# FFN's gate and up tiles as seven half products of summed halves, in a two-block kernel on one Trainium2 core

## The chip, the cores and the metric

The kernel runs on one core of a Trainium2 chip: TensorE (matrix products, PE), VectorE (DVE), ScalarE (ACT), GpSimd (POOL), SyncE (SP, which here only issues DMAs), on-chip memory (SBUF), and eight accumulation banks of 128 x 512 fp32 that TensorE writes (PSUM). The metric is the device time of one execution in microseconds (us), without the profiler; lower is better.

## The reference

Two transformer-like blocks in float32 on x of [1, 512, 1024]: first a convolution branch, a differential attention and a cross attention, merged and projected; then a second block with gated mixing, a recurrent time mix, and FFN. Only FFN is touched:

```
x = layer_norm_2(ALPHA * x + gt1 * mix, ln1_g, ln1_b)
h = x * (1.0 + sc2) + sh2                     # [512, 1024]
gu = h @ w_ffn_in                             # [512, 2 * 2816]
f = (silu(gu[..., :2816]) * gu[..., 2816:]) @ w_ffn_out
x = layer_norm_2(ALPHA * x + gt2 * f, ln2_g, ln2_b)
```

## The kernel before, in words

Every large product is kept near fp32 by a split. An fp32 operand is rounded to the type fp32r (its hi part, by a ScalarE copy), and the rest, operand minus hi, is a second fp32r tile (its lo part, by a VectorE subtraction). `mm3` (lines 583 to 585) then issues three matmuls, hi x hi, hi x lo and lo x hi, into one bank.

Weights come as units of 128 x 1024 fp32 (512 KB) in the order of a written-out plan, through four `raw` slots; SyncE loads a slot again when its unit's lo part is done. `feed_hi` and `feed_lo` (lines 625 and 633) split the units in turn into three pairs of parts (SPLIT = 3), each freed when the product that used it is done. The engines run written-out instruction orders and wait on semaphores; a `Ring` hands out banks and scratch tiles in turn and waits for the last reader of each. Each engine takes its instructions strictly in its own order, so an instruction that waits holds all behind it.

FFN has 22 pairs of tiles. Pair n is the unit ffn_g n and the unit ffn_u n, each the 128 columns of one tile for all 1024 inputs (KT = 8 slices of 128 x 128). For each, TensorE multiplies the 8 slices with the 8 slices of h3_T (h transposed, hi and lo, 512 tokens): 24 matmuls of 512 columns into one bank of a ring of three (`units`). Pair 0 is computed in halves of 256 tokens while h3_T is still being turned (`first_units`). ScalarE takes the gate with Silu into a scratch tile, VectorE multiplies it by the up bank in place, ScalarE rounds the result (hidden hi, line 2152), VectorE makes its rest (hidden lo, line 2174). At n = 10 TensorE also makes gate rows (line 1492), which take two banks of the same ring; their input tiles come from `dve_diagonals` (line 2825). In pairs 2 to 5 VectorE also applies the first row norm's gains and biases (`dve_gain_rows`).

Then come 22 output products, one per unit ffn_out n: VectorE scales the raw weights by the gate rows (line 661), they are split, and TensorE adds 24 matmuls of 512 columns (4 token tiles x 2 halves x 3) into all eight banks, which stay taken until the end. The last three units are ordered by token tile, and the last norm runs behind it.

The modulated rows of h (h3) pass through three scratch tiles (`modulated_ring`), where ScalarE writes them, rounds them, and VectorE makes the rest. GpSimd does nothing in FFN but issue eight DMAs of norm rows.

Of the kernel before, what the change touches and what calls it, by code (L numbers as in the profile page):

```python
# [14 lines left out]
P = 128  # L15
# [30 lines left out]
HEAD_STEPS = {6: 1, 7: 3, 8: 2, 9: 2, 10: 2, 11: 2, 12: 2, 13: 2, 14: 2}  # L46
ROW_SPOT = {"emb": "even", "ln1": "odd", "ln2": "even", "sg": "sg"}
# [229 lines left out]
def build(nc, dram, out):  # L277
# [3 lines left out]
    in_turn = [u for u in weights_of if plan[u][0] not in EARLY]  # L281
# [161 lines left out]
    wide = bank_ring((0, 1, 2, 4, 5, 6, 7))  # L443
    half_places, last_places = bank_ring((0, 1, 2, 3)), bank_ring((3, 4, 5, 6, 7, 0, 1, 2))
# [13 lines left out]
    act_ring, modulated_ring = place_ring((0, 1, 2, 3)), place_ring((2, 3, 4))  # L458
# [3 lines left out]
    final_ring = place_ring((), (scratch[7], *scratch[0:4]))  # L462
    f_logw, f_wall, f_total, s_sq = scratch[0], scratch[3], scratch[5], scratch[4:6]
# [106 lines left out]
    hidden_hi, hidden_lo = signal("ffn_hi"), signal("ffn_lo")  # L570
# [40 lines left out]
    def feed_hi(act, count=1):  # L611
        for _ in range(count):
            n = progress["hi"]
            if n == len(weights_of):
                return
            progress["hi"] += 1
            u = weights_of[n]
            act.wait_ge(*(weight_scaled.at(u) if plan[u][0][0] == "ffn_out" else raw_loaded[u % RAW].at(u)))
# [2380 lines left out]
```

## Time and profile before

| what | us |
|---|---|
| median of 3 runs without the profiler | 1617.43 (1616.83 to 1620.52) |
| profiled execution: span from first to last instruction | 1726.6 |
| profiled execution: its time outside the span | not given |
| TensorE matmuls busy in the span | 1692.6 (98%) |
| TensorE weight loads busy | 1289.1 (75%) |
| VectorE busy | 1001.7 (58%) |
| ScalarE busy | 718.1 (42%) |
| GpSimd busy | 189.8 (11%) |

A matmul's row lasts longer than its share of the engine, as matmuls overlap in the pipeline: distances between starts tell the pace. Names of tiles in the rows are the program's; a region of memory that is reused shows the first name it had, so that FFN's h3_T appears as h_T. The granted clock is the share of TensorE's full speed that the chip let it have.

### The profile page before, as it was taken

How to read it: one execution, taken by the hardware profiler on the slowest of the kernel's cores; microseconds unless marked ns; L12 is line 12 of the kernel's file. 1: busy time of each engine (PE TensorE's matmuls, PEld its weight loads, DVE VectorE, ACT ScalarE, POOL GpSimd, SP SyncE). 2: the span in 40 equal slices, each digit the busy share in tenths (PEclk: the TensorE clock that was granted, in tenths of full speed). 3: DMA queues.
4: the chain of work that ended last, by engine and by line, in shares of the span. 5: the costliest groups of instructions: out<-in, count | busy, mean ns of one | idle time of the engine just before them, and what ended most of it. 6: DMA issues, size and time to landing. Idle time of an engine off the chain costs nothing.

```text
span 1726.6 us, 24370 instructions
## 1 busy us (share of the span) xinstructions
PE 1692.6 (98%) x9964; PEld 1289.1 (75%) x9964; DVE 1001.7 (58%) x1684; ACT 718.1 (42%) x1151; POOL 189.8 (11%) x159
## 2 busy tenths in 40 slices
PE   7999999999999999999999999989999999999998
PEld 6777776777777777777777877778768777777776
DVE  5999884566554477656444737675446442334335
ACT  5544356334422476647522535553324222222112
POOL 2335364300010000000005000000000000000000
PEclk9888888888888888888888888888888888888888
DMA  5223243543454322232324132200012232222221
GB/s 200 89 84 117 79 134 103 179 133 123 146 174 134 110 90 82 75 108 86 122 86 154 57 97 74 85 4 4 3 49 98 85 110 85 86 86 90 93 85 49
DMA packets 45645, 166.07 MB, mean 96 GB/s; under 512 B 5264, under 2 KB 5392, under 8 KB 45536
## 3 DMA queue, kind: packets, MB, share of 16 engines
q1 hardware_dynamic: 42912, 155.95, 28.3%
q0 software_dynamic: 2624, 8.59, 1.7%
q8 instruction: 79, 1.29, 0.3%
q14 instruction: 30, 0.25, 0.0%
HBM read 162.42 MB, written 2.10 MB: 95 GB/s over the span
## 4 chain that ended last, share of the span: by engine, by line
PE 93%; DVE 4%; ACT 2%; issue 1%; DMA 0%; SPq 0%; DVEq 0%; ACTq 0%
PE bank L583 28%; PE bank L584 27%; PE bank L585 27%; PE bank L1287 2%; PE bank L1139 1%; PE bank L1118 1%; DVE small L2195 1%; PE bank L900 1%; ACT scratch L594 0%; PE bank L1459 0%; PE bank L1134 0%; PE bank L1385 0%; PE bank L1338 0%; DVE x_rows L2169 0%; PE bank L1280 0%
## 5 line engine op out<-in xcount | busy, mean ns | idle before, releaser
L583 PE MATMUL bank<-h_T_hi,weight_hi 128*128 128x512 f32 (+1 forms) x1184 | 505.1, 427 | 1.1 <-DVE scratch L2166 1.1
L625 ACT ACTIVATE weight_hi<-raw 128x1024 fp32r<-128x1024 f32 x237 | 250.3, 1057 | 613.9 <-PE bank L585 613.8
L633 DVE TENSOR_TENSOR weight_lo<-raw,weight_hi 128x1024 fp32r<-128x1024 f32 x180 | 220.2, 1225 | 470.4 <-ACT weight_hi L625 470.3
L584 PE MATMUL bank<-h_T_lo,weight_hi 128*128 128x512 f32 (+1 forms) x1184 | 492.4, 416 | 0.0
L585 PE MATMUL bank<-h_T_hi,weight_lo 128*128 128x512 f32 (+1 forms) x1184 | 492.1, 416 | 0.0
L583 PEld LDWEIGHTS bank<-h_T_hi,weight_hi 128*128 128x128 f32 x1184 | 229.0, 193 | 76.7 <-issue 10.0
L584 PEld LDWEIGHTS bank<-h_T_lo,weight_hi 128*128 128x128 f32 x1184 | 228.7, 193 | 67.6 <-issue 4.5
L585 PEld LDWEIGHTS bank<-h_T_hi,weight_lo 128*128 128x128 f32 x1184 | 227.7, 192 | 68.4
L2169 DVE SCALAR_TENSOR_TENSOR bank<-conv_in,columns,bank 128x512 f32<-128x512 f32 x240 | 181.4, 756 | 8.3
L633 POOL TENSOR_TENSOR weight_lo<-raw,weight_hi 128x1024 fp32r<-128x1024 f32 x57 | 139.1, 2440 | 177.5 <-ACT weight_hi L625 177.5
L583 PE MATMUL bank<-branch_hi,weight_hi 128*128 128x512 f32 x192 | 81.1, 422 | 0.0
L585 PE MATMUL bank<-branch_hi,weight_lo 128*128 128x512 f32 x192 | 80.3, 418 | 0.0
L584 PE MATMUL bank<-branch_lo,weight_hi 128*128 128x512 f32 x192 | 80.1, 417 | 0.0
L584 PE MATMUL bank<-weight_lo,hidden_hi 128*128 128x512 f32 x176 | 73.7, 419 | 0.0
L583 PE MATMUL bank<-weight_hi,hidden_hi 128*128 128x512 f32 x176 | 73.5, 417 | 0.0
L585 PE MATMUL bank<-weight_hi,hidden_lo 128*128 128x512 f32 x176 | 73.0, 415 | 0.0
L583 PE MATMUL bank<-weight_hi,h_T_hi 128*128 128x512 f32 x160 | 66.9, 418 | 0.0
L585 PE MATMUL bank<-weight_hi,h_T_lo 128*128 128x512 f32 x160 | 66.8, 417 | 0.0
L584 PE MATMUL bank<-weight_lo,h_T_hi 128*128 128x512 f32 x160 | 66.6, 416 | 0.0
L646 DVE SCALAR_TENSOR_TENSOR raw<-raw,silu_row 128x1024 f32<-128x1024 f32 x48 | 60.4, 1260 | 0.0
L594 ACT ACT_TABLE_LOAD x43 | 55.2, 1283 | 6.5 <-PE bank L1257 3.0
L791 POOL DMA_DIRECT2D ln_rows<-in_ln_g x4 | 2.2, 546 | 399.3 <-DVE scratch L2166 319.9
(453 smaller groups left out, 2415.9 us busy)
## 6 DMA issues: line engine op xcount, KB each, us to landing
raw<-in_weights SPq DMA_DIRECT2D x289, 512.0 KB, 3.5
x_in<-in_x SPq DMA_DIRECT2D x4, 512.0 KB, 5.2
x_rows<-in_x POOLq DMA_DIRECT2D x4, 512.0 KB, 4.9
out<-x_rows SPq DMA_DIRECT2D x4, 512.0 KB, 2.6
mem_in<-in_mem POOLq DMA_DIRECT2D x2, 512.0 KB, 4.4
ln_rows<-in_ln_g POOLq DMA_DIRECT2D x4, 256.0 KB, 3.8
ln_rows<-in_ln_b POOLq DMA_DIRECT2D x4, 256.0 KB, 4.5
silu_row<-in_c POOLq DMA_DIRECT2D x1, 512.0 KB, 6.2
```

The source lines that it names most:

```text
L583: pe.matmul(o, lhs[0], rhs[0], start=start, stop=False)
L584: pe.matmul(o, lhs[0], rhs[1], start=False, stop=False)
L585: return pe.matmul(o, lhs[1], rhs[0], start=False, stop=stop)
L594: return act.activation(o, i, func, bias=bias, scale=scale)
L625: act.activation(weight_parts(u)[0][:, :], raw[u % RAW][:, :], ACT.Copy).then_inc(*weight_hi.up(u))
L633: engine.tensor_tensor(lo[:, :], raw[u % RAW][:, :], view(hi[:, :]), ALU.subtract).then_inc(*ready.up(u))
L646: dve.scalar_tensor_tensor(out=slot, in0=slot, scalar=1.0, in1=silu_row[:, :], op0=ALU.mult, op1=ALU.mult, accum_out=mod[:, v, k:k + 1]).t ...
L900: done = pe.transpose(turned_bank(what, g, k)[:, cut(n)], tiles[2 * g + n][:, cut(k)], ident[:, :])
L1118: done = pe.transpose(bank[:, cut(j)], s_ring["s", h, t, 0][:, cut(j)], ident[:, :])
L1139: pe.matmul(bank, ones_head[:, :], norm_ring_d[what, h], start=True, stop=True).then_inc(*norm_sum.up(what, h))
L1287: return pe.matmul(bank[lanes, cut(m, CHUNK)], lhs(m, rows), rhs(m, rows), start=start, stop=start or m == 7)
L2169: return dve.scalar_tensor_tensor(out=o, in0=a, scalar=scalar, in1=b, op0=op0, op1=op1)
```

## The change

Pairs 0 and 1 stay as they are (DIRECT = 2). In each of the pairs 2 to 21 the work is seen as a product of 2 x 2 blocks: the inputs in two halves of 512 (4 slices each), the tokens in two halves of 256 (`firsts`, `lasts`), and gate and up as the two output halves. It is computed with seven block products of sums in place of eight plain ones. Each block product ("step") is 4 slices x 3 matmuls of 256 columns.

- Sums of activations, once: GpSimd builds S1 to S4 (each 128 x 4 x 256) from h3, which is therefore kept in full in `h3_full` in place of the ring; ScalarE and VectorE split each.
- Sums of weights, per pair: GpSimd makes T1 to T4 (128 x 512 each) from the four raw halves. Seven parts of 512 columns (B11, B21, B22, T1 to T4) are split by ScalarE and VectorE, for pair n+1 during pair n, each behind the step that used it. Six lie in the three weight slots, B22 in a tile of its own.
- TensorE runs P1, P6, P7, P2, P5, P4, P3. P2 adds onto P1's bank after ScalarE has copied P1 (`first_copy`); P3 adds onto P5's bank after VectorE has read it (C22). The steps use banks 0, 1, 2, 4, 5; the gate rows now use banks 6 and 7 and move to n = 12.
- VectorE forms the sums of results in five additions of 256 columns (U2, U3, C22, C21, C12) and multiplies gate by up. ScalarE's Silu runs in two halves.
- The hidden tiles stay in fp32. They are rounded and their rests made in the output stage, the first four (HI_AHEAD) in pair 21. Rest and full tile share memory; the hi parts lie where the activation sums were.
- The first norm's gains move to pairs 2 to 9, one half per pair; the diagonals to n = 11; SyncE's wait before a reload becomes T4 and the rest of B21 or B22 of the pair that left.

```diff
+STEPS = ("P1", "P6", "P7", "P2", "P5", "P4", "P3")
+PART_OF = {"P1": "B11", "P6": "T2", "P7": "T3", "P2": "B21", "P5": "T1", "P4": "T4", "P3": "B22"}
+SUM_OF = {"P6": "S2", "P7": "S3", "P5": "S1", "P3": "S4"}
+FREES_SLOT = ("P6", "P2", "P4")
...
+    def pool_weight_sums(pool, n):
...
+        def difference(name, a, b):
+            if n > DIRECT:
+                pool.wait_ge(*part_lo.at(n - 1, name))
+            pool.tensor_tensor(weight_sums[name][:, :], a, b, ALU.subtract).then_inc(*weight_summed.up(n, name))
+        difference("T1", b12, b11)
+        pool.wait_ge(*weight_summed.at(n, "T1"))
+        difference("T2", b22, weight_sums["T1"][:, :])
+        difference("T3", b22, b12)
+        pool.wait_ge(*weight_summed.at(n, "T2"))
+        difference("T4", b21, weight_sums["T2"][:, :])
...
+    def pe_sevens(pe, n):
...
+        def product_of(step, bank, start=True):
+            hi, lo = seven_parts[PART_OF[step]]
+            pe.wait_ge(*part_lo.at(n, PART_OF[step]))
+            if n == DIRECT and step in SUM_OF:
+                pe.wait_ge(*sum_lo.at(SUM_OF[step]))
+            for k in range(KT // 2):
+                done = mm3(pe, bank[:, 0:M], (hi[:, cut(k)], lo[:, cut(k)]), moving(step, k), start and k == 0,
+                           k == KT // 2 - 1, not start)
+            done.then_inc(*seventh.up(n, step))
+        first = seven_places["C11"].take(pe, n, seven_act, n, "C11")
+        product_of("P1", first)
+        product_of("P6", seven_places["P6"].take(pe, n, seven_dve, n, "U2"))
+        product_of("P7", seven_places["P7"].take(pe, n, seven_dve, n, "U3"))
+        pe.wait_ge(*seven_act.at(n, "P1"))
+        product_of("P2", first, start=False)
+        fifth = seven_places["P5"].take(pe, n, seven_dve, n, "C12")
+        product_of("P5", fifth)
+        product_of("P4", seven_places["P4"].take(pe, n, seven_dve, n, "C21"))
+        pe.wait_ge(*seven_dve.at(n, "C22"))
+        product_of("P3", fifth, start=False)
...
+    def act_sevens(act, n):
+        gate = act_ring.take(act, ("ffn", n), hidden_done, n)
+        def later(step):
+            if n + 1 < FT:
+                act_part(act, n + 1, PART_OF[step])
+            elif step in FREES_SLOT:
+                feed_hi(act)
+        act.wait_ge(*seventh.at(n, "P1"))
...
+        act.activation(first_copy, seven_places["C11"][n][:, 0:M], ACT.Copy).then_inc(*seven_act.up(n, "P1"))
+        later("P1")
+        later("P6")
+        later("P7")
+        act.wait_ge(*seventh.at(n, "P2"))
+        activate(act, gate[:, firsts], seven_places["C11"][n][:, 0:M], ACT.Silu).then_inc(*seven_act.up(n, "C11"))
+        later("P2")
+        later("P5")
+        if n == FT - 1:
+            for early in range(HI_AHEAD):
+                act_hidden_hi(act, early)
+        later("P4")
+        act.wait_ge(*seven_dve.at(n, "C21"))
+        activate(act, gate[:, lasts], gate_half, ACT.Silu).then_inc(*seven_act.up(n, "C21"))
+        later("P3")
...
+    def dve_sevens(dve, n):
...
+        later("P1")
+        added("U2", second_sum, first_copy, "P6", seven_act.at(n, "P1"))
+        later("P6")
+        added("U3", third_sum, second_sum, "P7", seven_dve.at(n, "U2"))
+        later("P7")
+        if n - DIRECT < 2 * TT:
+            t, half = divmod(n - DIRECT, 2)
+            dve_gain_rows(dve, "ln1", t, half, ln_rows).then_inc(*moved.up("ln1", t, half))
+        later("P2")
+        added("C22", up[:, lasts], third_sum, "P5", seven_dve.at(n, "U3"))
+        later("P5")
+        added("C21", gate_half, third_sum, "P4", *([seven_act.at(n - 1, "C21")] if n > DIRECT else []))
+        later("P4")
+        if n == FT - 1:
+            for early in range(HI_AHEAD):
+                dve_hidden_lo(dve, early)
+        added("C12", up[:, firsts], second_sum, "P3")
...
+        mult(dve, hidden[n][:, :], up[:, :], act_ring["ffn", n]).then_inc(*hidden_done.up(n))
+        later("P3")
...
     def dve_ffn(dve):
+        dve_part(dve, DIRECT, "B11")
+        dve_part(dve, DIRECT, "T2")
+        dve_sum(dve, "S1")
+        dve_direct(dve, 0)
+        for name in ("S2", "S3", "S4"):
+            dve_sum(dve, name)
+        dve_direct(dve, 1)
+        for name in ("T3", "B21", "T1", "T4", "B22"):
+            dve_part(dve, DIRECT, name)
...
+        for n in range(DIRECT, FT):
+            if n == 11:
+                dve_diagonals(dve, 5)
+            if n == FT - 1:
+                dve_scale(dve, index["ffn_out", 0])
+            dve_sevens(dve, n)
+        for n in range(HI_AHEAD, FT):
+            feed_lo(dve)
+            dve_hidden_lo(dve, n)
```

## Rows read from the trace of the kernel before

**Rows 1.** The page: busy time of the engines, chain by engine.
```profile
PE 1692.6 (98%) x9964; PEld 1289.1 (75%) x9964; DVE 1001.7 (58%) x1684; ACT 718.1 (42%) x1151; POOL 189.8 (11%) x159
...
PE 93%; DVE 4%; ACT 2%; issue 1%; DMA 0%; SPq 0%; DVEq 0%; ACTq 0%
```
**Rows 2.** Busy time by stretches, FFN's pairs and output products; last: clock, DMA.
```profile
core 0: us, PE busy (x) PEld busy (x) DVE busy (x) ACT busy (x) POOL busy (x), PEclk, DMA share, GB/s
1330.00:1571.30 241.30, 240.22 (x956) 183.09 (x955) 84.92 (x105) 66.55 (x83) 2.16 (x4) 0.85 0.29 92
...
1586.30:1719.00 132.70, 132.62 (x529) 101.20 (x527) 60.44 (x87) 28.34 (x34) 0.00 (x0) 0.85 0.23 72
```
**Rows 3.** Timeline (start, length, instruction): TensorE in FFN, two matmuls 48 apart.
```profile
1375.27 0.41 PE L583 MATMUL bank<-h_T_hi,weight_hi 128*128 128x512 f32 x1
...
1387.31 0.41 PE L583 MATMUL bank<-h_T_hi,weight_hi 128*128 128x512 f32 x1
```
**Rows 4.** Timeline: TensorE in cross attention, first of 12 half-width matmuls and the next.
```profile
348.30 0.30 PE L583 MATMUL bank<-k_x_hi,q_x_hi 128*128 128x256 f32 x1
...
349.80 0.42 PE L583 MATMUL bank<-h_T_hi,weight_hi 128*128 128x512 f32 x1
```
**Rows 5.** Busy time by stretches: around rows 4.
```profile
348.00:350.00 2.00, 2.00 (x15) 1.89 (x14) 0.89 (x2) 0.23 (x1) 0.00 (x0) 0.85 0.53 109
```
**Rows 6.** Timeline: TensorE's weight loads in the stretch of rows 4.
```profile
348.43 0.19 PEld L585 LDWEIGHTS bank<-k_x_hi,q_x_lo 128*128 128x128 f32 x1
348.55 0.20 PEld L583 LDWEIGHTS bank<-k_x_hi,q_x_hi 128*128 128x128 f32 x1
```
**Rows 7.** Timeline: ScalarE at FFN's start.
```profile
1324.16 0.58 ACT L594 ACTIVATE scratch<-bank,fold 128x256 f32<-128x256 f32 x1
...
1332.69 0.63 ACT L2152 ACTIVATE hidden_hi<-scratch 128x512 fp32r<-128x512 f32 x1 [0.81 <-DVE scratch L2166]
...
1337.36 0.58 ACT L594 ACTIVATE scratch<-bank 128x512 f32<-128x512 f32 x1
1342.42 1.06 ACT L625 ACTIVATE weight_hi<-raw 128x1024 fp32r<-128x1024 f32 x1 [4.48 <-PE bank L585]
```
**Rows 8.** Timeline: VectorE at FFN's start.
```profile
1324.32 0.43 DVE L2174 TENSOR_TENSOR h_T_lo<-scratch,h_T_hi 128x256 fp32r<-128x256 f32 x1 [0.33 <-ACT h_T_hi L1954]
...
1337.49 1.23 DVE L633 TENSOR_TENSOR weight_lo<-raw,weight_hi 128x1024 fp32r<-128x1024 f32 x1 [4.83 <-ACT weight_hi L625]
1338.63 0.69 DVE L2174 TENSOR_TENSOR hidden_lo<-scratch,hidden_hi 128x512 fp32r<-128x512 f32 x1
```
**Rows 9.** Timeline: GpSimd's weight rests, alone and beside VectorE.
```profile
200.66 2.39 POOL L633 TENSOR_TENSOR weight_lo<-raw,weight_hi 128x1024 fp32r<-128x1024 f32 x1 [5.06 <-ACT weight_hi L625]
...
317.25 3.18 POOL L633 TENSOR_TENSOR weight_lo<-raw,weight_hi 128x1024 fp32r<-128x1024 f32 x1 [3.00 <-ACT weight_hi L625]
```
**Rows 10.** Groups by form (count, busy us, mean ns): GpSimd's 128-wide tensor_tensor.
```profile
L767 POOL TENSOR_TENSOR wide_levels<-wide_levels,ident 128x128 f32<-128x128 f32 x5 | 2.1, 459 | 0.1
```
**Rows 11.** Timeline: TensorE, the turning of h, and the first matmul of pair 2.
```profile
1317.78 3.15 PE L900 MATMUL bank<-ident,x_rows 128*128 128x128 f32 x15 [2.00 <-DVE x_rows L2206]
...
1342.16 0.41 PE L583 MATMUL bank<-h_T_hi,weight_hi 128*128 128x512 f32 x1
```
**Rows 12.** DMA issues in FFN's pairs: count, size, us to landing.
```profile
raw<-in_weights SPq DMA_DIRECT2D x40, 512.0 KB, 3.5
```
**Rows 13.** Timeline: VectorE beside the second of rows 9.
```profile
316.95 1.22 DVE L646 SCALAR_TENSOR_TENSOR raw<-raw,silu_row 128x1024 f32<-128x1024 f32 x1
...
318.10 0.69 DVE L2166 TENSOR_TENSOR y_T<-bank,y_T 128x512 f32<-128x512 f32 x1
318.70 2.81 DVE L646 SCALAR_TENSOR_TENSOR raw<-raw,silu_row 128x1024 f32<-128x1024 f32 x1
```
**Rows 14.** Waits from 1430 to 1450 us: in total, times, longest.
```profile
PE bank L583 <- DVE scratch L2166: 1.1, 1, 1.1
```
**Rows 15.** Timeline: VectorE scales an output unit.
```profile
1590.79 1.29 DVE L661 TENSOR_TENSOR raw<-raw,scratch 128x512 f32<-128x512 f32 x2
```
**Rows 16.** Busy time by stretches, as rows 2: behind TensorE's idle time before 1317.78.
```profile
1318.00:1320.00 2.00, 2.00 (x12) 1.81 (x11) 1.16 (x4) 1.91 (x5) 0.00 (x0) 0.53 0.86 289
```

More of the change, by code:

```diff
@@ L462, in build @@
     final_ring = place_ring((), (scratch[7], *scratch[0:4]))
+    firsts, lasts = slice(0, M), slice(M, S)
+    slots = [parts[(turn_of[index["ffn_out", 0]] + n) % SPLIT] for n in range(SPLIT)]
+    seven_parts = {}
+    for slot, pair in zip(slots, (("B11", "T2"), ("T3", "B21"), ("T1", "T4"))):
+        for half, name in enumerate(pair):
+            seven_parts[name] = tuple(t[:, half * S:(half + 1) * S] for t in slot)
+    seven_parts["B22"] = tuple(t[:, :] for t in last_part)
     f_logw, f_wall, f_total, s_sq = scratch[0], scratch[3], scratch[5], scratch[4:6]
@@ L1486, in pe_rwkv, with gate_banks @@
                     lambda f: pe_states(pe, f), lambda: pe_out_steps(pe), lambda v: pe_gate_rows(pe, v))
+    def gate_banks(v):
+        return units if v == 2 else gate_places
     def pe_gate_rows(pe, v):
         for half in range(2):
-            bank = units.take(pe, ("gate", v, half), gate_row, v, half)
+            bank = gate_banks(v).take(pe, ("gate", v, half), gate_row, v, half)
             pe.wait_ge(*diagonal.at(v, half))
@@ L2142, in act_ffn @@
     def act_ffn(act):
         act_rows(act, "ln1", h3_T[0], 1)
-        for n in range(FT):
-            if n:
-                feed_hi(act)
-            gate = act_ring.take(act, ("ffn", n), hidden_lo, n)
-            act_take(act, ("ffn_g", n), gate, ACT.Silu)
-            if n:
-                feed_hi(act)
-            act.wait_ge(*taken["dve"].at("ffn_u", n))
-            act.activation(hidden[n][0][:, :], gate, ACT.Copy).then_inc(*hidden_hi.up(n))
-            if n == 9:
+        act_part(act, DIRECT, "B11")
@@ new lines, in dve_part, with dve_direct, later, added @@
+    def dve_part(dve, n, part):
+        hi, lo = seven_parts[part]
+        dve_rest(dve, lo, part_source(n, part), hi, part_hi.at(n, part)).then_inc(*part_lo.up(n, part))
+    def dve_direct(dve, n):
+        dve.wait_ge(*taken["act"].at("ffn_g", n))
+        dve.wait_ge(*product.at("ffn_u", n))
+        mult(dve, hidden[n][:, :], units["ffn_u", n], act_ring["ffn", n]).then_inc(*taken["dve"].up("ffn_u", n))
+    def dve_sevens(dve, n):
+        up = up_tiles[n % 2]
+        def later(step):
+            if n + 1 < FT:
+                dve_part(dve, n + 1, PART_OF[step])
+            elif step in FREES_SLOT:
+                feed_lo(dve)
+        def added(name, o, a, step, *free):
+            dve.wait_ge(*seventh.at(n, step))
+            for wait in free:
+                dve.wait_ge(*wait)
+            bank = seven_places[{"P3": "P5"}.get(step, step)][n]
+            dve.tensor_tensor(o, a, bank[:, 0:M], ALU.add).then_inc(*seven_dve.up(n, name))
+        later("P1")
[15 more added lines that the diff above has]
+        added("C12", up[:, firsts], second_sum, "P3")
+        dve.wait_ge(*seven_act.at(n, "C21"))
+        dve.wait_ge(*seven_dve.at(n, "C12"))
+        mult(dve, hidden[n][:, :], up[:, :], act_ring["ffn", n]).then_inc(*hidden_done.up(n))
+        later("P3")
```

190 lines of the change are left out of this document (148 added, 42 removed).

## The prediction

> **What bounds the kernel now.** I read the page's busy times and chain first, then busy time by stretches, then timelines. [rows 1]: TensorE's matmuls are busy 98% of the span and make 93% of the chain that ended last. [rows 2] narrows this to FFN: from 1330.0 us (pair 1, the unit before the changed ones) on, TensorE is idle 1.1 us in 241.3, and the output products run as densely, while VectorE is busy 84.9 of 241.3, ScalarE 66.6 and GpSimd 2.2. A matmul removed there is time removed, until the side engines, which the change loads heavily, can't follow.
>
> [rows 3] are two matmuls 48 apart: one gate/up pair (8 x 3 matmuls, twice) takes 12.04 us, 0.251 us per 512 columns. The "0.41" of a row is its length in the pipeline, not its pitch.
>
> The sums are made in the profiled execution. Its span is 1726.6 us, its time outside it isn't given, and the median without the profiler is 1617.43, 0.937 of the span. TensorE being the bound, I take it that TensorE's work shrinks by 0.937 and that of the others doesn't.
>
> **What a half product costs.** A changed pair issues 7 x 4 x 3 = 84 matmuls of 256 columns in place of 96 halves. Do 256 columns take half of 0.251, though each still loads 128x128 weights? [rows 4]: in the cross-attention scores the matmuls at 348.30 and 349.80 are 12 apart: 1.50 us, 0.125 each, at the granted clock of FFN, 0.85 [rows 5]. The weight loads [rows 6] start 0.13 us apart though one lasts 0.19 (busy 1.89 of 2.00 us there): they overlap each other and the matmuls. So a step of 12 is 1.506 us, a pair 7 x 1.506 = 10.54, and 20 pairs give 20 x (12.05 - 10.54) = **-30.1 us**.
>
> The Trainium skill speaks against this ("TensorE: Matmul & The Clock Gate", section The mechanism): a weight load overlaps running matmuls only when it goes to another row group, and these all use the full array; its section on LDWEIGHTS gives 107 ns for one. By that rule a half matmul would cost an estimated 107 + 107 ns and a full one 107 + 213, so 84 against 48 is 2.6 us more per pair. The trace disagrees: 1.50 us for 12 leaves no room for a load.
>
> **The side engines' work.** ScalarE [rows 7]: rounding 512 wide 0.63, from PSUM 256 wide 0.58, Silu 512 wide 0.58, a half one at most that. VectorE [rows 8]: 512 wide 0.69 (0.61 where the next follows at once), 256 wide 0.42 (0.36). Per pair VectorE does 7 weight rests, the product, and five 256-wide adds: 8 x 0.61 + 5 x 0.36 = 6.7 us, and 1.2 more in the first eight pairs, for the gains of one row half. ScalarE: 7 roundings (4.4), first_copy and two half Silus (1.7): 6.1. GpSimd had no 512-wide tensor_tensor; 1024 wide took 2.39 [rows 9], 128 wide 0.46 [rows 10]; a line through both gives 1.29 for 512, of which 1.10 is data and 0.19 fixed. Bounds 1.20 (half of 2.39) and 1.59 (half of 3.18). Four are 5.2 us.
>
> **Order, without contention.** In pair n, with P1 issued at 0, step i issues its last matmul at 1.51 i, and a taker starts 0.26 later (ScalarE's 1342.42 in [rows 7] after the next unit's first matmul, 1342.16 in [rows 11]). Each part for pair n+1 is made right after its step of pair n, six steps ahead of need. Tight is P3, which goes onto P5's bank once C22 is read: P2 is out at 6.28; ScalarE's half Silu and rounding of B21 end at 7.4; VectorE's rest of B21 at 8.0, C22 at 8.45; P3 is due at 9.04. Slack 0.6. P2 needs first_copy at 2.35 and issues at 4.5. GpSimd's T1 to T4 start when T1's rest is done, at 9.2, for the pair after next, and T2 is wanted by ScalarE only at 3.3 of the next. The load of the up weights is issued at 2.0 (behind B22's rest), lands 3.5 later [rows 12], and is wanted at 9.2. All covered.
>
> **GpSimd against VectorE.** [rows 9] and [rows 13] show one meeting. VectorE's 1024-wide operation with two SBUF inputs runs from 316.95 for 1.22; GpSimd's tensor_tensor starts at 317.25 and takes 3.18, 0.79 over its 2.39, about what VectorE still had. VectorE's next such operation starts at 318.70, inside GpSimd's, and takes 2.81, 1.59 over 1.22, about what GpSimd still had (1.73). So the two shut each other out; which of them is held is a matter of who came first. The add at 318.10, with one operand in PSUM, also starts inside GpSimd's and takes its 0.69: the five adds of a pair are free of it.
>
> The Trainium skill ("SBUF — State Buffer", section Who interferes with whom) says that only the pair of ports that VectorE shares with GpSimd causes contention, as an exclusive lock, and that two SBUF inputs take part in it. The trace agrees with its 1.59 us.
>
> In a changed pair, seven rests and the product meet four GpSimd operations that hold the port 1.1 us each. From 9.25 on: T1 holds it to 10.45, T4's rest waits 0.4; T2 holds it to 12.15, the product waits 0.65; then T3 and B22's rest want it together, then T4 and B11's rest. If GpSimd wins both (2.2 us), VectorE reaches C22 at 8.63 of the next pair, just in time; if VectorE wins, earlier. With the gains' 1.2 us it is 9.85: late by 0.8 in eight pairs. That is VectorE's loop: 6.7 + 3.3 of waiting = 10.0 (11.2 with gains) against TensorE's 10.54. Without the profiler TensorE's pair is 10.54 x 0.937 = 9.87, and the loop, with 0.1 of hand-overs, 10.1 and 11.3: 12 x 0.2 + 8 x 1.4 = 13.6 us; if VectorE wins, 0 to 2. I take the middle, **+7.5**; bounds 0 and, at 0.2 us longer holds (4 x 0.2 x 20), 30.
>
> **The head.** h3_full takes the ring's place with no wait; TensorE runs densely here already, so nothing is gained. GpSimd starts S1 when the last modulated tile is done, 1324.7 [rows 7]; S1 to S4 take 2.4 each and the wait for S1's rest: 1334.5, rounding and rest 2.3 more. They are wanted from 1343.7 (P6 of pair 2): covered. But pair 1's up product ends at 1342.2 [rows 11], VectorE multiplies to 1343.15 and only then makes the rests of T3, B21 and T1 (1345.0). GpSimd may overwrite T1 only then, and T3 of pair 3 is out at 1348.9, 1350.1 with contention. Behind T3's rest in VectorE's queue stand two gain operations, B21's rest and C22: 1348.9 + 0.63 + 0.1 + 0.69 + 1.3 + 0.65 + 0.45 = 1352.7, with contention 1354.5, while P3 is due at 1351.2: 1.5 to 3.3 late, **+3.0**, once.
>
> **The gate rows.** Before, the gate matmuls took banks of the gate/up ring, and TensorE then stood 1.1 us for VectorE [rows 14]. Now they have banks 6 and 7: **-1.1**.
>
> **The tail.** In pair 21 no parts are made and GpSimd is done; VectorE scales and splits output weights instead: scaling 1.29 [rows 15], rest 1.15 (1.23 alone, [rows 8]). From 2.05: scale 0 to 3.35, U2, scale 1 to 5.05, rest 0 to 6.2, U3, scale 2 to 7.85, rest 1 to 9.0, C22 to 9.4: P3 late, **+0.5**. Then C21 9.75, scale 3 11.05, rest 2 12.2, four hidden rests 14.65, and only then C12, 15.05. P3 has ended by 11. The output product needs hidden rest 0 (12.85), works 0.75 us in bank 3 and wants bank 4, which C12 still holds. TensorE stands 15.1 - 11.0 - 0.75 = **+3.4** (bounds 1.5, if only the first wait counts, and 5). Behind such idle time the granted clock falls: idle 2.0 us before 1317.78 [rows 11], then 0.53 in place of 0.85 [rows 16]. 3.4 us of it cost **+1.4** (bounds 0 and 2.8, as pair 2's stall may do it too). In the output stage a product takes 6.0 us, VectorE's load per product rises to 3.1, ScalarE's to 1.7: hidden, as VectorE was busy 60 of 133 [rows 2].
>
> **Sum**: (-30.1 - 1.1) x 0.937 = -29.2; + 7.5 + 3.0 + 0.5 + 3.4 + 1.4 = -13.4: **1604.0 us**.
>
> **Rivals.**
> A. VectorE wins the port or its waits fall into idle time, and TensorE stays the bound: no +7.5, 1596.5. For: GpSimd needs a hand-over between its operations. Against: two ties in a row, and no row shows one. 0.22.
> B. Slower: VectorE's loop through the shared port becomes the bound in every pair. It does when GpSimd's operations come near 1.6, or hold the port for their whole length. At 11.3 and 12.7 us a pair 12 x 11.3 + 8 x 12.7 = 237 against 12.05 x 20 x 0.937 = 226: +11, with head and tail 8.3 less the gate rows' 1.0: +18, 1636. It decides from about 10.9 a pair. For: VectorE's loop lies within 3% of TensorE's pair. Against: GpSimd's row at 2.39. 0.15.
> C. C22 is late through its five hand-overs, not the port: 0.5 us in each pair besides, 1614. Each is a row, against it. 0.06.
> D. Matmuls bound by weight loads: at 0.19 a load 84 take 16.0, +3.9 a pair, 1690. Against it [rows 4], the same shape. It or a loss that I don't see: 0.03.
> The forecast has 0.54.
>
> **Range.** Nothing late but the tail's first wait gives 1590; the upper half of the forecast's port cost with the upper bounds of tail and clock 1614. The forecast's own range is 1597 to 1613; with A and the near part of B and C, 1591 to 1620. Faster by over 0.2% (3.2 us, about what this kernel's measurement can tell): forecast, A and half of C, 0.78. Within 0.2%: 0.07, where B and C begin. Slower 0.15.
>
> **What would show it.** Matmul pitch 0.125; pairs 10 to 20 near 10.6 us from P1 to P1, pairs 3 to 9 longer, with TensorE waiting before P3 for VectorE's C22; rests of T4, B22, B11 and the product well above 0.69 beside GpSimd's operations; one idle of 1.5 to 3.3 us before P3 of pair 2; two idles around the first output products, released by VectorE, with a dip of the clock behind. No idle before P3 would show A, one in every pair with stretched rests B, one with rests at 0.69 C, a pitch above 0.13 D.

## The result and the profile after

The changed kernel is slower: 1631.91 us (median of 4 runs, 1630.42 to 1635.82) against 1618.34 (4 runs, 1616.83 to 1620.52). The ratio is 1.0089, 95% interval 1.0075 to 1.0103. The forecast was 1604.0, with 1620 as its upper end. Medians and ratios in this document leave out two disturbed executions, one of 2532.61 us (the new order of pair 21) and one of 4527.29 us (the four edits together).

The page of the changed kernel's profile, busy times and chain, answers to [rows 1]:

```profile
span 1633.9 us, 26614 instructions
...
PE 1555.3 (95%) x10684; PEld 1280.6 (78%) x10684; DVE 1155.5 (71%) x1888; ACT 772.1 (47%) x1295; POOL 326.1 (20%) x243
...
PE 63%; DVE 26%; ACT 6%; issue 4%; DMA 0%; SPq 0%; DVEq 0%; ACTq 0%
```

TensorE's share of the chain fell from 93% to 63%, VectorE's rose from 4% to 26%. Busy time by stretches (columns as in [rows 2]) shows the pairs 2 to 21 and the output products:

```profile
1270.60:1495.80 225.20, 205.99 (x1673) 201.66 (x1671) 218.60 (x289) 108.89 (x203) 122.44 (x80) 0.96 0.33 101
1501.20:1625.00 123.80, 123.77 (x525) 99.60 (x525) 68.07 (x100) 35.80 (x50) 0.00 (x0) 0.99 0.23 73
```

In the pairs VectorE is busy 218.6 of 225.2 us, TensorE 206.0: the bound has moved. A pair without gains on VectorE (timeline; [rows 8] has the same 512-wide rest alone):

```profile
1453.64 0.68 DVE L2370 TENSOR_TENSOR weight_lo<-weight_sum_T,weight_hi 128x512 fp32r<-128x512 f32 x1
1454.24 0.41 DVE L3079 TENSOR_TENSOR scratch<-scratch,bank 128x256 f32<-128x256 f32 x1
1454.57 1.75 DVE L2370 TENSOR_TENSOR weight_lo<-weight_sum_T,weight_hi 128x512 fp32r<-128x512 f32 x1
1456.25 0.41 DVE L3079 TENSOR_TENSOR scratch<-scratch,bank 128x256 f32<-128x256 f32 x1
1456.76 1.27 DVE L2362 TENSOR_TENSOR hidden<-scratch,scratch 128x512 f32<-128x512 f32 x1
1457.96 1.78 DVE L2370 TENSOR_TENSOR last_part_lo<-raw,last_part_hi 128x512 fp32r<-128x512 f32 x1
1459.66 1.79 DVE L2370 TENSOR_TENSOR weight_lo<-raw,weight_hi 128x512 fp32r<-128x512 f32 x1
...
1464.17 0.68 DVE L2370 TENSOR_TENSOR weight_lo<-weight_sum_T,weight_hi 128x512 fp32r<-128x512 f32 x1
```

and on GpSimd:

```profile
1454.49 1.29 POOL L871 TENSOR_TENSOR weight_sum_T<-raw,raw 128x512 f32<-128x512 f32 x1 [4.12 <-DVE weight_lo L2370]
1455.86 1.63 POOL L871 TENSOR_TENSOR weight_sum_T<-raw,weight_sum_T 128x512 f32<-128x512 f32 x1
1457.44 1.74 POOL L871 TENSOR_TENSOR weight_sum_T<-raw 128x512 f32<-128x512 f32 x1
1459.14 1.75 POOL L871 TENSOR_TENSOR weight_sum_T<-raw,weight_sum_T 128x512 f32<-128x512 f32 x1
```

All four large VectorE operations beside GpSimd's T1 to T4 are stretched: T4's rest 1.75, the product 1.27, B22's and B11's rests 1.78 and 1.79, where 0.68 is one alone. The adds, with an operand in PSUM, keep 0.41. Each stretched operation starts inside one of GpSimd's and ends 0.54 to 0.56 us after it; GpSimd's next is then longer by 0.3 to 0.5. The two take turns. From T1's rest (1453.64) to the next pair's (1464.17) is 10.53 us, with only 0.1 us of idle time in it (before the product). TensorE waits for it, before P3, in every pair:

```profile
1453.77 0.38 PE L625 MATMUL bank<-sum_S_hi,last_part_hi 128*128 128x256 f32 x1 [0.67 <-DVE scratch L3079]
```

Outside the pairs three places are late: the turning of h (TensorE, timeline; the kernel before, at full clock, stands 2.69 and 0.61 us there), P3 of pair 2, and the first output products.

```profile
1243.69 0.98 PE L996 MATMUL bank<-ident,x_rows 128*128 128x128 f32 x7 [3.88 <-DVE x_rows L2402]
1246.51 1.12 PE L996 MATMUL bank<-ident,x_rows 128*128 128x128 f32 x4 [1.83 <-DVE h_T_lo L2370]
...
1283.06 0.58 PE L625 MATMUL bank<-sum_S_hi,last_part_hi 128*128 128x256 f32 x1 [3.83 <-DVE scratch L3079]
...
1499.14 0.47 PE L625 MATMUL bank<-weight_hi,hidden_hi 128*128 128x512 f32 x1 [1.62 <-DVE weight_lo L677]
1501.23 0.79 PE L625 MATMUL bank<-weight_hi,hidden_hi 128*128 128x512 f32 x1 [1.15 <-DVE scratch L3079]
```

The row at 1499.14 puts the wait down to the rest of output weights (L677), which ended at 1498.44; hidden rest 0, behind it in VectorE's queue, ended at about 1499.0 and was the last that the product needed.

### The profile page after: what moved, and what is told of

It is laid out like the page before. It is cut to its first block, busy times and chain, and to the rows that moved or that the text cites. A ratio compares the mean times of both kernels' runs of the same rounds, so it can differ in the third digit from the quotient of the medians.

```text
span 1633.9 us, 26614 instructions
## 1 busy us (share of the span) xinstructions
PE 1555.3 (95%) x10684; PEld 1280.6 (78%) x10684; DVE 1155.5 (71%) x1888; ACT 772.1 (47%) x1295; POOL 326.1 (20%) x243
## 4 chain that ended last, share of the span: by engine, by line
PE 63%; DVE 26%; ACT 6%; issue 4%; DMA 0%; SPq 0%; DVEq 0%; ACTq 0%
PE bank L625 19%; PE bank L626 18%; PE bank L627 18%; DVE bank L2365 8%; DVE weight_lo L2370 2%; PE bank L1383 2%; DVE weight_lo L677 1%; DVE scratch L3079 1%; ACT weight_hi L669 1%; DVE scratch L2365 1%; DVE scratch L2362 1%; ACT scratch L636 1%; DVE small L2391 1%; DVE h_T_lo L2370 1%; DVE x_rows L2365 1%
## 5 line engine op out<-in xcount | busy, mean ns | idle before, releaser
L625 PE MATMUL bank<-h_T_hi,weight_hi 128*128 128x512 f32 (+1 forms) x1104 | 419.2, 380 | 1.5 <-DVE conv_in L2362 0.9
L627 PE MATMUL bank<-h_T_hi,weight_lo 128*128 128x512 f32 (+1 forms) x1104 | 406.5, 368 | 0.0
L626 PE MATMUL bank<-h_T_lo,weight_hi 128*128 128x512 f32 (+1 forms) x1104 | 406.2, 368 | 0.0
L677 DVE TENSOR_TENSOR weight_lo<-raw,weight_hi 128x1024 fp32r<-128x1024 f32 x140 | 173.5, 1241 | 258.5 <-ACT weight_hi L669 258.4
L677 POOL TENSOR_TENSOR weight_lo<-raw,weight_hi 128x1024 fp32r<-128x1024 f32 x57 | 140.0, 2457 | 155.1 <-ACT weight_hi L669 155.0
L2297 ACT ACTIVATE weight_hi<-weight_sum_T 128x512 fp32r<-128x512 f32 x80 | 50.3, 632 | 52.7 <-PE bank L627 48.1
L2370 DVE TENSOR_TENSOR weight_lo<-weight_sum_T,weight_hi 128x512 fp32r<-128x512 f32 x80 | 73.9, 925 | 1.6 <-ACT weight_hi L2297 1.6
L627 PE MATMUL bank<-weight_hi,hidden_rest 128*128 128x512 f32 x176 | 70.1, 398 | 0.0
L871 POOL TENSOR_TENSOR weight_sum_T<-raw,weight_sum_T 128x512 f32<-128x512 f32 x40 | 67.0, 1675 | 1.6
L625 PE MATMUL bank<-sum_S_hi,weight_hi 128*128 128x256 f32 x240 | 66.7, 278 | 0.0
L627 PE MATMUL bank<-sum_S_hi,weight_lo 128*128 128x256 f32 x240 | 66.7, 278 | 0.0
L626 PE MATMUL bank<-sum_S_lo,weight_hi 128*128 128x256 f32 x240 | 66.7, 278 | 0.0
```

Of the source, the lines that this page charges most:

```text
L625: pe.matmul(o, lhs[0], rhs[0], start=start, stop=False, skip_group_check=onto)
L626: pe.matmul(o, lhs[0], rhs[1], start=False, stop=False, skip_group_check=onto)
L627: return pe.matmul(o, lhs[1], rhs[0], start=False, stop=stop, skip_group_check=onto)
L677: engine.tensor_tensor(lo[:, :], raw[u % RAW][:, :], view(hi[:, :]), ALU.subtract).then_inc(*ready.up(u))
L871: pool.tensor_tensor(weight_sums[name][:, :], a, b, ALU.subtract).then_inc(*weight_summed.up(n, name))
L2297: act.activation(seven_parts[part][0], part_source(n, part), ACT.Copy).then_inc(*part_hi.up(n, part))
```

## The experiments

Times are medians; "before" is the kernel before on the same chip in the same job. I call the distance between the starts of two P3 a pair's time, and "the way in" the stretch from y_b's last product to pair 2 (y_b is an input of the projection just before h is turned). The wait before a P3 is given from the start of P4's last matmul to the start of P3; 0.12 us of it is the usual distance of two matmuls, and the idle time in brackets in a row is about 0.28 shorter. T1(2) is T1 of pair 2.

**Before again, for its profile.** [rows 1 to 16] come from an execution at a clock of 0.85.

> The kernel before, unchanged, for its trace at the clock that its timed runs have (the trace that the prediction was worked out from had a granted clock of 0.85, that of the changed kernel 0.98). If the clock alone made that trace longer, the span is about 1616 us at a clock near 0.98, and a gate/up pair takes 11.1 to 11.3 us from first matmul to first matmul; output products 5.6. If the profiler lengthened it, the clock is again 0.85 and the span 1727.

Span 1618.0 us, clock 0.994, 1619.75 in all. Two matmuls 48 apart, as in [rows 3]:

```profile
1361.09 0.39 PE L583 MATMUL bank<-h_T_hi,weight_hi 128*128 128x512 f32 x1
...
1372.08 0.39 PE L583 MATMUL bank<-h_T_hi,weight_hi 128*128 128x512 f32 x1
```

A pair takes 10.99 us. The spans of the two traces differ by 108.6 us; the kernel and the profiler are the same, the granted clock is not. By stage, the changed kernel (span 15.9 us longer) loses 3.1 before y_b's last product (this point lies at 1231.3 to 1236.8 in the twelve traces of this study, whose code up to there hardly differs, so that is scatter), 4.5 on the way in (34.16 against 29.68), 5.45 in pair 2 up to the first output product (228.54 against 223.09), 2.8 in the output products, 0 after.

**GpSimd's sums 8 columns wide, and memsets in their place.** The same number of GpSimd operations with the same waits, from pair 3 on; the rest of each sum keeps its old values.

```
+            w = S if n == DIRECT else 8
-            pool.tensor_tensor(weight_sums[name][:, :], a, b, ALU.subtract)...
+            pool.tensor_tensor(weight_sums[name][:, 0:w], a[:, 0:w], b[:, 0:w], ALU.subtract)...
```

> GpSimd's four weight sums of a pair are 8 columns wide from pair 3 on (the sums are then stale, everything else is done): same waits, same instructions, almost no time at the shared port. Port theory: VectorE's rests fall back to 0.69 us and a pair to TensorE's 9.6 us in place of 10.5 (11.8 in the pairs with gains): 1632 - 18 x 1.6 = about 1602 us. Rival 'VectorE's own work and the hand-overs between three engines': pairs stay at 10.5 and 11.8, 1630 us. Rival 'head and tail alone': the same, 1630.

1601.41 (before 1616.87), ratio 0.9897, 0.9869 to 0.9925. Pairs 9.60, no idle before P3 in pairs 3 to 20. VectorE's timeline: the product and B22's rest as alone, and GpSimd's short sum:

```profile
1426.18 0.69 DVE L2363 TENSOR_TENSOR hidden<-scratch,scratch 128x512 f32<-128x512 f32 x1
1426.79 0.68 DVE L2371 TENSOR_TENSOR last_part_lo<-raw,last_part_hi 128x512 fp32r<-128x512 f32 x1
...
1424.44 0.20 POOL L872 TENSOR_TENSOR weight_sum_T<-raw,raw 128x8 f32<-128x8 f32 x1 [8.06 <-DVE weight_lo L2371]
```

With two memsets in place of each sum, so that the sums are left out:

```
+            if n > DIRECT:
+                pool.memset(weight_sums[name][:, :], 0.25).then_inc(*pool_own.up())
+                pool.wait_ge(*pool_own.last())
+                pool.memset(weight_sums[name][:, :], 0.5).then_inc(*weight_summed.up(n, name))
+                return
```

> From pair 3 on GpSimd writes a constant twice in place of each weight sum (sums are then wrong): about as long on GpSimd (two times 0.54 us and a hand-over), but nothing is read. If it is GpSimd's reads that hold VectorE: rests at 0.69, pairs at 9.6, about 1602 us like the 8-column version. If it is the length of GpSimd's chain, or its writes: pairs stay at 10.5 and 11.8, 1630 us.

1604.40 (ratio 0.9915, 0.9889 to 0.9941), pairs 9.60 again, though GpSimd is now busy 21.4 of 60 us in the pairs and writes the same tiles (stretch and timeline):

```profile
1400.00:1460.00 60.00, 60.00 (x528) 60.00 (x527) 46.34 (x84) 32.34 (x61) 21.37 (x42) 1.00 0.35 115
```

```profile
1427.13 0.53 POOL L874 MEMSET weight_sum_T<- 128x512 f32 x1
...
1427.14 0.69 DVE L2367 TENSOR_TENSOR hidden<-scratch,scratch 128x512 f32<-128x512 f32 x1
```

The product starts 0.01 us after a memset and takes its 0.69. The memsets and their hand-over are a little shorter than the sums they replace (two of 0.53 against 1.29 alone). So neither GpSimd's waits nor its writes cost the pairs, and hardly its length: what costs is GpSimd's tensor_tensor, with its two reads, running beside VectorE. From pair 2's start to the first output product the 8-wide version takes 197.39 us, 31.15 less than the changed kernel: 3.7 of it at P3 of pair 2 (wait 4.10 against 0.40), **27.5 in the pairs after it**.

**T1 to T4 on VectorE, from pair 4 on.**

```
         for n in range(DIRECT + 1, FT):
+            if n <= BY_POOL:                         # 3
                 pool_weight_sums(pool, n)
...
         later("P5")
+        dve_weight_sum(dve, n + 2, "T1")
         added("C21", gate_half, third_sum, "P4", ...)
+        dve_weight_sum(dve, n + 2, "T2")
         later("P4")
+        dve_weight_sum(dve, n + 2, "T3")
...
         mult(dve, hidden[n][:, :], up[:, :], act_ring["ffn", n])...
+        dve_weight_sum(dve, n + 2, "T4")
```

> VectorE itself makes T1 to T4 from pair 4 on (4 x 0.61 = 2.4 us more per pair), GpSimd is idle. Port theory: the loop is 6.7 + 2.4 = 9.1 us (10.3 with gains) with nothing to wait for, so pairs of 9.6 to 9.9 (10.4 to 10.7 with gains), 1608 us. Rival 'VectorE's own work': its loop was 10.5 and 11.8 and grows by 2.4 to 12.9 and 14.2, 1675 us.

1613.41, ratio 0.9974 (0.9957 to 0.9990), 5 us short of what I expected, but the pairs are as expected: 9.60, with gains 10.62. In the same place of a gains pair:

```profile
1336.44 0.69 DVE L876 TENSOR_TENSOR weight_sum_T<-raw 128x512 f32<-128x512 f32 x1
1337.04 0.42 DVE L3103 TENSOR_TENSOR scratch<-scratch,bank 128x256 f32<-128x256 f32 x1
1337.56 0.69 DVE L2386 TENSOR_TENSOR hidden<-scratch,scratch 128x512 f32<-128x512 f32 x1
1338.17 0.69 DVE L876 TENSOR_TENSOR weight_sum_T<-raw,weight_sum_T 128x512 f32<-128x512 f32 x1
```

A sum costs VectorE 0.61 if VectorE makes it, and on average 1.0 if GpSimd does (the four meetings above add 1.07, 0.59, 1.10 and 1.11 to 0.68). The help cost more than the work it took over. The way in, with GpSimd's sums for pairs 2 and 3, is untouched here (34.16 us, and P3 of pair 2 waits 4.10), which I had left out of the expectation.

**The gains in the output stage.** VectorE's part in the pairs smaller by 1.2 us in eight pairs, GpSimd's sums left.

```
-        if n - DIRECT < 2 * TT:                      # in dve_sevens
+            if n - HI_AHEAD < 2 * TT:                # in the loop behind the pairs
...
                 dve_gain_rows(dve, "ln1", t, half, ln_rows)...
```

GpSimd's issue of the second norm's rows moves behind its last sum with it.

> One edit to the changed kernel: the first norm's gains leave pairs 2 to 9 for the output stage, one row half behind each of the hidden rests 4 to 11 (VectorE has some 2.5 us free per output product). Port theory: VectorE's loop is the bound, so these pairs fall from 11.8 to 10.5 us, and the wait before P3 of pair 2 by the gains' 1.3: 1632 - 8 x 1.25 - 1 = 1621 us. Rival 'only head and tail made it slower, the pairs are TensorE's': 0 to -1, 1631.

1624.31, ratio 1.0044 (1.0029 to 1.0058). The pairs went from 11.84 to 10.52 us and P3's wait in pair 2 from 4.10 to 2.78, each by the 1.3 us that two gain operations take. Two distances were longer, 12.04 and 13.29: `dve_diagonals` (n = 11) stands there without slack, and the second also holds the gate rows, which alone take 2.04 in the 8-wide version. In the changed kernel the same two are 11.70 and 11.74, so 1.9 of the 3 us by which the time missed 1621 are there.

**The new order of pair 21.**

```
-        later("P4")
         if n == FT - 1:
-            for early in range(HI_AHEAD):
+            dve_hidden_lo(dve, 0)
+        else:
+            later("P4")
+        added("C12", up[:, firsts], second_sum, "P3")
+        if n == FT - 1:
+            later("P4")
+            for early in range(1, HI_AHEAD):
                 dve_hidden_lo(dve, early)
-        added("C12", up[:, firsts], second_sum, "P3")
```

> One edit to the changed kernel, in pair 21 alone: VectorE makes hidden rest 0 and then C12 before it scales output weights 3 and makes the rests of output weights 2 and hidden tiles 1 to 3. The two idle times of TensorE around the first output products (1.9 and 1.6 us) should go, and the fall of the clock behind them (3.4 us at half speed, 1.7 us): 1632 - 3.2 - 1.7 = 1627 us. If the waits have another cause (the weights' rests), they stay and the time with them, 1632.

1629.41, ratio 1.0077 (1.0059 to 1.0094), against 1.0089 (1.0075 to 1.0103) for the changed kernel. In its trace the stage did what was expected:

```profile
1493.88 0.39 PE L625 MATMUL bank<-sum_S_hi,last_part_hi 128*128 128x256 f32 x1 [0.63 <-DVE scratch L3079]
1495.41 0.40 PE L625 MATMUL bank<-weight_hi,hidden_hi 128*128 128x512 f32 x1
```

From the last P3 to the first output product 1.53 us (3.31 before), and first to last output product 123.04 (125.75): 4.5 us in the trace. That hidden rest 0 and C12 caused the two idle times is shown by this. The times say less: 0.12% or some 2 us better, with intervals that overlap, so that neither the expected 4.9 us nor nothing is excluded.

**The way in.** In the changed kernel GpSimd's T1(2) starts at 1241.80, beside VectorE's last row centring (timelines of the changed kernel, and of before again):

```profile
1241.63 2.01 DVE L2402 TENSOR_SCALAR x_rows<-x_rows,small 128x1024 f32<-128x1024 f32 x1 [0.60 <-ACT small L636]
1241.80 1.28 POOL L871 TENSOR_TENSOR weight_sum_T<-raw,raw 128x512 f32<-128x512 f32 x1
```

```profile
1238.49 0.81 DVE L2206 TENSOR_SCALAR x_rows<-x_rows,small 128x1024 f32<-128x1024 f32 x1 [0.60 <-ACT small L594]
```

The turning then waits for centring and rests. The first version moves the T(2) sums behind S1 (ScalarE's rounding of T2 likewise).

```
-        pool_weight_sums(pool, DIRECT)               # ahead of S1
         pool.tensor_tensor(s1, a21, a22, ALU.add)
+        pool_weight_sums(pool, DIRECT)
...
-        dve_part(dve, DIRECT, "T2")
         dve_sum(dve, "S1")
         dve_direct(dve, 0)
+        dve_part(dve, DIRECT, "T2")
         for name in ("S2", "S3", "S4"):
             dve_sum(dve, name)
+        for name in ("T3", "B21"):
+            dve_part(dve, DIRECT, name)
         dve_direct(dve, 1)
```

> Two moves in the changed kernel before pair 2: GpSimd's T1 to T4 for pair 2 come behind S1, out of the stage where h is turned, and VectorE makes the rests of T3 and B21 before its product of pair 1. Port theory: the turning stage loses the 1.2 us by which VectorE's row centring is held (2.01 in place of 0.81) and the stretched rests, in all about 3 of the 3.7 us that it grew; the wait before P3 of pair 2 falls from 4.1 by about 1.2: 1628 us. Rival 'the stage grew because ScalarE writes h3_full and not the ring': the stage stays, 1631.

1633.44, ratio 1.0093 (1.0078 to 1.0108): a miss. y_b's last product to the last transpose fell from 12.51 us to 8.91 (before: 8.78), though ScalarE still writes `h3_full`: the rival is out, and GpSimd's sums were what had stretched the turning. But pair 2 began only 32.81 us after y_b, and P6 in it waited again. All four edits together:

> All together: VectorE makes T1 to T4 from pair 4 on, gains in the output stage, the tail's order, the head's order. VectorE's loop is 9.1 us, under TensorE's 9.6: 20 pairs of 9.6 and no waits at the tail. 1617 (before) - 20 x (11.0 - 9.6) - 1 (gate rows' wait) + 2 (pair 2's wait) = about 1590 us. If it stays above 1600, something besides the port holds the pairs.

1600.92, ratio 0.9893 (0.9876 to 0.9909): 11 us above the expectation. The pairs are 9.60. TensorE stands before P1 and P6 of pair 2 (timeline; then busy time by stretches, columns as in [rows 2], right behind the second wait):

```profile
1265.01 0.39 PE L626 MATMUL bank<-h_T_hi,weight_hi 128*128 128x256 f32 x1 [2.57 <-ACT scratch L637]
...
1268.60 0.58 PE L626 MATMUL bank<-sum_S_hi,weight_hi 128*128 128x256 f32 x1 [1.39 <-DVE hidden L2385]
```

```profile
1268.60:1273.40 4.80, 4.80 (x25) 4.80 (x26) 4.80 (x6) 0.63 (x1) 4.01 (x3) 0.57 0.56 144
```

Start to start the two waits are 2.97 and 1.8 us. Behind them the granted clock was 0.57, so that they cost more than their length: pair 1 took 13.82 and pair 2 14.04 in place of 10.99 and 9.60, 7.3 us where I had allowed 2. The pair with the diagonals is 1.0 long. Of the 11 us some 5 stay unplaced.

Both waits look like banks given back late. The next two versions are this one without its edit of the way in, and with the two give-backs moved forward:

> VectorE makes T1 to T4 from pair 4 on, the gains stand in the output stage, and pair 21 has its new order; the turning stage is as in the changed kernel. It is the four-edit version without its edit of pair 2's way in, so the difference of the two is that edit, measured where no wait later in FFN can hide it. By the port theory the pairs after 3 take 9.60 us and the turning stage is the changed kernel's: its last transpose comes 12.5 us after the last product of y_b (8.8 in the four-edit version), and no idle of 2.97 us before P1 of pair 2. From pair 1 to pair 2 it then takes 11.1 us in place of 13.8: +3.7 - 2.8 and the second wait of 1.8 gone, but the wait before P3 of pair 2 back at 2.8: about 1603, within 2 of the four-edit version. If the port had nothing to do with the turning stage, its last transpose would come within 9 us and the time would be 1597.

1602.66, ratio 0.9906 (0.9893 to 0.9919), as expected: the way in is the changed kernel's (34.19), with P3 of pair 2 waiting 3.09.

```
-        for name in ("S2", "S3", "S4"):
-            dve_sum(dve, name)
-        for name in ("T3", "B21"):
-            dve_part(dve, DIRECT, name)
-        dve_direct(dve, 1)
+        dve_sum(dve, "S2")
+        dve_direct(dve, 1)
+        dve_sum(dve, "S3")
+        for name in ("T3", "B21"):
+            dve_part(dve, DIRECT, name)
+        dve_sum(dve, "S4")
```

> The four-edit version with another order inside pair 2's way in: ScalarE takes ffn_g 1 out of its bank ahead of the rounding of S2, and VectorE forms the product of ffn_u 1 right behind S2's rest, with T3 and B21's rests behind S3's and S4's behind those. The idle of 2.97 us before P1 of pair 2 ended in the four-edit version 0.05 us after ScalarE's move of ffn_g 1, which stood behind the rounding of S4, and that of 1.8 us before P6 was for the bank of ffn_u 1. Theory: both were banks given back late, nothing of the products' data: both idles go, pair 1 to pair 2 takes 11.0 to 11.3 us in place of 13.8, at most 1 us comes back before P7 or P3, and the time is 1597 to 1599. Rival: the sums S2 to S4 on GpSimd were late in themselves, because the four T(2) sums stand ahead of them (S2 started 7.3 us after S1's end): then the idle only moves to P6, P7 and P3 of pair 2 and the time stays at 1601 to 1602.

1605.22 (1600.04 to 1608.27; the trace is of one at 1600.66), ratio 0.9921 (0.9905 to 0.9936). The waits before P1 and P6 went as the theory said; the gain didn't come, as the rival said, for the idle moved to P3:

```profile
1272.37 0.63 ACT L2320 ACTIVATE weight_hi<-weight_sum_T 128x512 fp32r<-128x512 f32 x1 [6.66 <-POOL weight_sum_T L893]
...
1276.78 0.58 PE L626 MATMUL bank<-sum_S_hi,last_part_hi 128*128 128x256 f32 x1 [5.09 <-DVE scratch L3105]
```

ScalarE stood 6.66 us for T2(3), and C22 came behind that. In all three orders (four edits, three, this one) GpSimd starts on T(3) 36.9 to 37.1 us after y_b's last product, when VectorE has made the rest of T1(2), and P3 of pair 2 starts 45.3 to 45.5 us after it. Pair 2's end lies at 46.8, 46.8 and 48.2; behind the longer idle of the last the granted clock was 0.50 (1276.8 to 1279.5), and 1.00 in P3 of the other two. None of these orders helped. The last run gives every sum to VectorE, on top of the three edits:

```
         norm_rows("ln1")
-        pool_weight_sums(pool, DIRECT)
-        pool_sums(pool)
...
+        dve_weight_sum(dve, DIRECT, "T1")
+        dve_weight_sum(dve, DIRECT, "T2")
+        dve_full_sum(dve, "S1")
         dve_part(dve, DIRECT, "B11")
         dve_part(dve, DIRECT, "T2")
+        dve_full_sum(dve, "S2")
         dve_sum(dve, "S1")
         dve_direct(dve, 0)
-        for name in ("S2", "S3", "S4"):
-            dve_sum(dve, name)
+        dve_full_sum(dve, "S3")
+        dve_weight_sum(dve, DIRECT, "T3")
+        dve_sum(dve, "S2")
+        dve_full_sum(dve, "S4")
+        dve_weight_sum(dve, DIRECT, "T4")
+        dve_sum(dve, "S3")
         dve_direct(dve, 1)
```

Behind it come the rests of pair 2's parts and of S4, with T1 to T4 of pair 3 between them.

> As three_edits, with every sum on VectorE: the four of pairs 2 and 3 and h3's S1 to S4 too, so that GpSimd adds nothing between y_b and the output stage (ScalarE takes ffn_g 1 ahead of the rounding of S3). In the three versions of the way in that ran, the last product of y_b and the end of pair 2 lie 46.8 to 48.2 us apart whatever the order, which would be 39 to 40 without a wait. Port theory: VectorE's stream through this stretch is what sets it, because each GpSimd sum costs it 1.1 to 2.2 us beside it, while the sum itself costs VectorE 0.69 (512 wide) or 1.2 to 1.3 (1024 wide); after the turning stage VectorE then has 2.5 (two slots) + 1.4 (two products) + 4.1 (six parts) + 4.9 (rests of S1 to S4) + 4.9 (the sums) + 5.5 (eight weight sums) = 23.3 us of work, against some 29 us from its start to P3 of pair 2. The turning stage is back at 8.8 us, pair 2 starts 29.7 us after y_b, its waits together are at most 2 us, pair 2 ends 39.5 to 41.5 us after y_b, and the time is 1595 to 1597. Rival: the chain of sum, rounding and rest itself sets it (S1, S2, S4 one after the other by three engines): then pair 2 still ends 45 us or more after y_b and the time stays at 1601 to 1603.

**1595.45** (before 1620.42), ratio 0.9854 (0.9835 to 0.9872): faster than both kernels, by 25 us and (across jobs) 36. VectorE does a 1024-wide sum in 1.22 us beside nothing. GpSimd took 2.39 to 3.40 for one in the versions before, and in the last of them VectorE's rest of S1 took 3.42 beside it:

```profile
1254.13 1.22 DVE L912 TENSOR_TENSOR full_sum_S<-full_sum_S,h_full 128x1024 f32<-128x1024 f32 x1
1255.27 1.22 DVE L2396 TENSOR_TENSOR sum_S_lo<-full_sum_S,sum_S_hi 128x1024 fp32r<-128x1024 f32 x1
```

The last transpose comes 7.8 us after y_b, pair 2 starts at 27.5, and ends at 41.65 (I had said 39.5 to 41.5), with one wait left, 3.36 us before its P3. That GpSimd's sums made the way in long is shown by this run, and so is that VectorE had room for them. It doesn't separate the port from GpSimd's own length: with VectorE the chain of sum, rounding and rest is shorter too (1.22 in place of 2.4 at least), and the run also takes ffn_g 1 out of its bank earlier. For the turning the port is the cause (0.81 against 2.01). That no order alone could have done it isn't shown, only that three didn't.

## Why the prediction was wrong, by its steps

**Half products: right.** At full clock 84 matmuls take 9.60 us where 48 took 10.99: -27.8 for 20 pairs, predicted -30.1 x 0.937 = -28.2. Their pitch is 0.114, half of the 0.229 of 512 columns. The gate rows lengthen their pair by 2.04 us in the 8-wide version and by 3.22 before (at full clock, TensorE's timeline, below): -1.2, predicted -1.1 x 0.937 = -1.0.

```profile
1350.88 1.88 PE L1492 MATMUL bank<-scratch,ones_all 128*128 128x512 f32 x4
1354.10 0.50 PE L583 MATMUL bank<-h_T_hi,weight_hi 128*128 128x512 f32 x1 [1.35 <-DVE scratch L2166]
```

**GpSimd against VectorE: the step that failed, mis-sized.** It named every place: the four meetings, the wait before P3 for C22, the pairs with gains longer. It gave +7.5; the measured cost is 27.5 (changed kernel less the 8-wide version). That is inside the term's own bounds, 0 and 30, but the stated range, with 1620 at its end, didn't carry that bound. Three parts make that up, for 12 pairs without gains and 8 with:
- I took the middle between two ways of deciding a tie. The figure for "GpSimd wins both", 13.6, was the one: +6.1. Nor was either a tie: the two take turns, and each of VectorE's four operations has one of GpSimd's in front of it.
- VectorE's loop was put at 10.1 and 11.3 and is 10.52 and 11.84: 12 x 0.42 + 8 x 0.54 = +9.4. The meetings cost 1.07, 0.59, 1.10 and 1.11 = 3.9 us in place of 3.3, T4's rest being held 1.07 and not 0.4 (it starts 0.08 after GpSimd's T1). These 0.6 are more than the 0.42: VectorE's own work was a little less than counted, save that the two gain operations take 1.3 and not 1.2. GpSimd's length alone, 1.29 from a line through [rows 9] and [rows 10], was exact; beside VectorE it was 1.63 to 1.75.
- TensorE's pair was put at 10.54 x 0.937 = 9.87 and is 9.60: 0.27 x 20 = +5.4 on what is exposed. The factor was the ratio of the whole kernel's times, but the stages differ: a pair went from 12.04 to 10.99, 0.913, the output products from 132.2 to 123.0, 0.930, all before y_b's last product by 0.940. Why they differ, no run here shows.

Together 28.4, against 27.5. The result is rival B's mechanism at a smaller size: VectorE's loop bounds every pair, at 10.52 and 11.84 where B needed 11.3 and 12.7. B named two conditions, operations near 1.6 or the port held for their whole length; beside VectorE the operations did take 1.63 to 1.75. I had argued against B with GpSimd's row alone (2.39) and given it 0.15; its own sentence that the loop lies within 3% of TensorE's pair was the stronger argument. The sign on record for B, an idle before P3 in every pair with stretched rests, is what the trace has. The Trainium skill ("SBUF — State Buffer", section Who interferes with whom) calls the shared ports an exclusive lock; these runs agree, with 0.68 against 1.78 us. I had weighed it as agreement and then let half of it go in the sum.

**The head: the right wait at P3 of pair 2, 1.0 us too short** (4.10, of which 3.7 go in the 8-wide version; predicted 3.0), **and a step was missing before it**: GpSimd's T(2) sums beside the turning of h (12.51 us against 8.78) and its sums S1 to S3 beside VectorE's rests, +4.5 on the way in. I asked only when S1 to S4 are wanted, not whom they hold up meanwhile.

**The tail: right.** Idle of 1.9 and 1.55 us before the first output product and in it, and a granted clock of 0.83 from 1496 to 1506: 1.9 before the first and 2.8 in the stage, 4.7 against 3.4 + 1.4 predicted; 0.8 before pair 21's P3 against 0.5.

**Sum.** 1604.0, plus 20.0 (port), 4.5 (way in), 1.0 (P3 of pair 2: 4.10 less the usual 0.12, against 3.0), 0.4 (half products), 0.2 (tail and P3 of pair 21), less 0.2 (gate rows), and plus 1.7 of scatter (3.1 ahead of FFN in the trace, less 2.3 by which the spans differ more than the medians, and 0.9 by which this job's before is above 1617.43): 1631.6, against 1631.91; that it meets so well is in part chance, for the parts hold to perhaps 1 us.

## What to carry to other kernels

Work given to GpSimd isn't free for VectorE: count each GpSimd operation that reads two SBUF operands at its full hold against VectorE's stream, in every stage that it overlaps, and compare with what VectorE would need to do it itself (here 0.61 against 1.0 us). When one engine's loop comes within a few per cent of another's, don't take the middle between two readings: compute each loop at the clock of an undisturbed run, and ask which of them a small error would put on top. And move a wait only when you know what stands behind it: two edits of the way in passed theirs on to a later step, and a wait of some us also costs the fall of the clock behind it.

## What the hardware showed that was not expected

- The two engines take turns, and VectorE's operation is held until the GpSimd operation that it meets has ended: VectorE's 512-wide operations of 0.68 us took 1.75 to 1.79 beside back-to-back GpSimd tensor_tensor, while GpSimd's own rose from 1.29 to 1.75 at most. Also a VectorE TENSOR_SCALAR with one SBUF tensor of 1024 columns was held (0.81 to 2.01 us).
- GpSimd's memset of the same tiles held nothing (a VectorE product of 0.69 beside one of 0.53).
- Behind waits of TensorE of 2.97 and 1.8 us the granted clock was 0.57 for 4.8 us; behind one of some 5 us it was 0.50 for 2.7 us. An idle of 0.67 us in every pair came with a mean of 1.00 in pairs late in the stage (1400 to 1460).
- A profiled execution of the same kernel may run at a clock of 0.85 or of 0.99 (spans of 1726.6 and 1618.0 us) while the medians of that kernel, job by job, lie between 1616.87 and 1620.42.
